# A two-layer hybrid decoder in float32 parts: the compression's first layer in plain float32 from a buffer of its own, two reorderings, and compressed operands padded to 128 rows

## The reference, cut to what matters

```python
def compress(kv, pos_emb, w1, w2, idx):          # 31 blocks of 32 tokens, stride 16
    blocks = kv[:, idx] + pos_emb[None, None, :, None, :]
    blocks = blocks.transpose(0, 1, 3, 2, 4).reshape(bsz, 31, 2, 32 * 64)
    return jax.nn.gelu(blocks @ w1) @ w2          # w1: 2048 x 128, w2: 128 x 64
...
kc, vc = compress(kc, ...), compress(vc, ...)
kc = apply_partial_rope(rms_norm(kc, k_norm[0]), cos_c, sin_c)
p_cmp = masked_softmax(einsum('bqghd,bngd->bghqn', q_c, kc) * scale, valid)
o_cmp = einsum('bghqn,bngd->bqghd', p_cmp, vc)
out   = g0 * o_cmp + g1 * o_slc + g2 * o_win      # o_slc, o_win: over the tokens
x     = x + concat([out, conv_part]) @ w_out
```

## Time and profile before

| | |
|---|---|
| median of three runs | 1798.89 us |
| the profiled execution | 1798.12 us, span 1796.3 us |
| PE busy | 1775.5 us, 99% of the span |
| PE weight loads | 1465.8 us, 82% |
| DVE | 859.3 us, 48% |
| ACT | 598.6 us, 33% |
| POOL | 92.5 us, 5% |
| granted TensorE clock | full in all 40 slices |
| chain that ended last | PE 95%, DVE 3%, ACT 1%, issue 1% |

### The profile page before, as it was taken

How to read it: one execution, slowest core, us unless ns; L and a number is a source line. 1 busy time by engine, 2 the same in 40 slices (tenths; PEclk the granted TensorE clock), 3 DMA queues, 4 the chain that set the end, 5 groups by cost and what they waited for, 6 DMA issues and landing times.

```text
span 1796.3 us, 22196 instructions
## 1 busy us (share of the span) xinstructions
PE 1775.5 (99%) x8164; PEld 1465.8 (82%) x8164; DVE 859.3 (48%) x1104; ACT 598.6 (33%) x838; POOL 92.5 (5%) x81
## 2 busy tenths in 40 slices
PE   8999999999999999999999999999999999999999
PEld 6888888877777878888888888888888888888887
DVE  5544443356788845444443344444432564444322
ACT  5333332235336534333222233232222533332211
POOL 0500000012000011000000000000000000000000
PEclk9999999999999999999999999999999999999999
DMA  6333343324320013333343323333432233333331
GB/s 177 94 93 99 99 115 97 89 75 104 83 82 13 1 47 94 96 102 93 93 125 96 95 82 94 102 96 93 124 97 66 77 94 98 101 93 107 113 96 47
DMA packets 321362, 163.68 MB, mean 91 GB/s; under 512 B 13893, under 2 KB 320041, under 8 KB 321322
## 3 DMA queue, kind: packets, MB, share of 16 engines
q1 hardware_dynamic: 321130, 163.08, 31.5%
q10 hardware_dynamic: 192, 0.08, 0.0%
HBM read 161.04 MB, written 2.10 MB: 91 GB/s over the span
## 4 chain that ended last, share of the span: by engine, by line
PE 95%; DVE 3%; ACT 1%; issue 1%; DMA 0%; SPq 0%; POOL 0%; ACTq 0%; DVEq 0%
PE ps_s L532 20%; PE ps_s L534 20%; PE ps_s L533 20%; PE ps_y L532 9%; PE ps_y L533 9%; PE ps_y L534 9%; PE ps_aux L867 2%; PE ps_y L850 1%; DVE w_lo L1407 1%; PE ps_s L818 1%; PE ps_aux L864 1%; ACT w_hi L1019 1%; PE ps_s L819 0%; PE ps_aux L869 0%; DMA x_in<-in_x 0%
## 5 line engine op out<-in xcount | busy, mean ns | idle before, releaser
L1407 DVE TENSOR_TENSOR w_lo<-raw,w_hi 128x1024 fp32r<-128x1024 f32 (+2 forms) x279 | 368.0, 1319 | 726.4 <-ACT w_hi L1019 725.9
L532 PE MATMUL ps_s<-xg_hi,w_hi 128*128 128x512 f32 x1576 | 618.8, 393 | 0.1
L534 PE MATMUL ps_s<-xg_hi,w_lo 128*128 128x512 f32 x1576 | 613.3, 389 | 0.0
L533 PE MATMUL ps_s<-xg_lo,w_hi 128*128 128x512 f32 x1576 | 613.3, 389 | 0.0
L1019 ACT CAST w_hi<-raw 128x1024 fp32r<-128x1024 f32 (+2 forms) x279 | 312.1, 1119 | 591.9 <-PE ps_s L534 298.1
L532 PEld LDWEIGHTS ps_s<-xg_hi,w_hi 128*128 128x128 f32 x1576 | 295.8, 188 | 65.8 <-issue 2.9
L533 PEld LDWEIGHTS ps_s<-xg_lo,w_hi 128*128 128x128 f32 x1576 | 295.9, 188 | 63.5 <-issue 2.4
L534 PEld LDWEIGHTS ps_s<-xg_hi,w_lo 128*128 128x128 f32 x1576 | 295.8, 188 | 61.9
L532 PE MATMUL ps_y<-act_hi,w_hi 128*128 128x512 f32 x704 | 274.3, 390 | 0.7 <-DVE w_lo L1407 0.7
L534 PE MATMUL ps_y<-act_hi,w_lo 128*128 128x512 f32 x704 | 273.9, 389 | 0.0
L533 PE MATMUL ps_y<-act_lo,w_hi 128*128 128x512 f32 x704 | 273.9, 389 | 0.0
(11 more groups left out here) (314 smaller groups left out, 1078.5 us busy)
## 6 DMA issues: line engine op xcount, KB each, us to landing
raw<-in_ffn_w_gate SPq DMA_DIRECT2D x88, 512.0 KB, 3.9
raw<-in_ffn_w_up SPq DMA_DIRECT2D x88, 512.0 KB, 3.9
raw<-in_ffn_w_down SPq DMA_DIRECT2D x64, 704.0 KB, 4.5
raw<-in_hyb_w_in SPq DMA_DIRECT2D x19, 512.0 KB, 3.8
x_in<-in_x SPq DMA_DIRECT2D x8, 256.0 KB, 6.0
raw<-in_hyb_cmp_w SPq DMA_DIRECT2D x4, 512.0 KB, 4.0
raw<-in_hyb_w_in SPq DMA_DIRECT2D x8, 256.0 KB, 3.3
raw<-in_hyb_w_out SPq DMA_DIRECT2D x16, 128.0 KB, 2.8
```

Source lines behind the costliest of these rows:

```text
L532: mm(bank, hi, x_hi, start=first, stop=False, **kw)
L533: mm(bank, hi, x_lo, start=False, stop=False, **kw)
L534: return mm(bank, lo, x_hi, start=False, stop=last, **kw)
L1407: tt(w_lo[:, n % 2, 0:size], raw[:, n % 4, 0:size], f32(w_hi[:, n % 2, 0:size]), ALU.subtract).then_inc(lo_ready, 1)
```

## The change

- `compress` reads w1 as it came from memory, in plain float32: 16 matmuls of 128x64 instead of 48 of 128x256. w1 has a buffer of its own, `w1_raw` (in the place of `pt_b`), and is loaded by four DMAs that wait for nothing on SP. The four units `U_W1` go, with their splits on ACT and DVE, and so do the splits of the operand (`split_blocks`, `blocks_low`). The units of the loop take their places in the order of splits.
- DVE: scaling and gain of key kw now come ahead of the rotation of ks.
- ACT, in `project_four`: the square of the query now comes ahead of the split of unit n+2 (in the fourth pass, root of kc and square both).
- `vc_t` and `ptc` have 128 rows instead of 32; POOL clears them once, the copies still write 32 rows, and the matmul of line 864 contracts over 128.
- The two small buffers `small` and `small_c` move behind `o_lo`. With that `o_hi` and `o_lo` (and `pt_even`, `pt_odd`) start 320 bytes past a multiple of 512.

```diff
-U_W1 = U_MIX + 7
-U_LOOP = U_W1 + 4
+U_LOOP = U_MIX + 7
...
-            vc_t = mb("vc_t", [NCP, P])
+            vc_t = mb("vc_t", [P, P])
-            ptc = mb("ptc", [NCP, T])
+            ptc = mb("ptc", [P, T])
-            small = mb("small", [P, 2, 10])          # now behind o_lo
-            small_c = mb("small_c", [P, 5, NQ])
-                pt_b = eb("pt_b", [P, 2, 4 * T], F32R)
+                w1_raw = eb("w1_raw", [P, 2, 2, KD * P])
...
# SP
-                load(U_W1 + u, 0, (slot(U_W1 + u), blocks_of(w1)))
+                sp.dma_start(w1_raw[:, u // 2, u % 2, :].rearrange("p (k f) -> p k f", f=P),
+                             blocks_of(w1)).then_inc(w1_landed[u // 2], 16)
...
# PE, compress(c)
-                pe.wait_ge(blk_lo_ready, c + 1)
+                pe.wait_ge(blk_step, 4 * (c + 1))
+                pe.wait_ge(w1_landed[c], 32)
                 for h in range(2):
-                    pe.wait_ge(lo_ready, n + 1)
                     for k in range(KD):
-                        last_mm = three(ps_s[:, p % 4, 0:8 * NCP], w_hi[...], w_lo[...], b_hi, b_lo, ...)
-                    last_mm.then_inc(unit_done, 1)
+                        at = c * 2 * T + (h * KD + k) * 2 * NCP
+                        last_mm = mm(ps_s[:, p % 4, 0:2 * NCP], w1_raw[:, c, h, k * P:(k + 1) * P], qf[:, at:at + 2 * NCP],
+                                     start=h == 0 and k == 0, stop=h == 1 and k == KD - 1)
+                last_mm.then_inc(compressed_by, 1)
...
# ACT
-            split(U_W1)
+            split(U_LOOP)
             split_keys(1)
-            split_blocks(0)
             take_values(0)
-            split(U_W1 + 1)
-            split_blocks(1)
+            split(U_LOOP + 1)
             take_values(1)
-            split(U_W1 + 2)
-            split(U_W1 + 3)
...
-            split(U_LOOP)
             tanh(0)
             split_hidden(0)
-            split(U_LOOP + 1)
             tanh(1)
...
-                    if not (u == 3 and b):
-                        split(n + 2, i)
                     if u == 0:
                         if b:
                             root("kc", DH, 2 * NCP)
                         act.wait_ge(proj_scaled, 10 + 4 * b + 4 * i)
                         square("q3" if b else "q0", sq[:, :], work[:, 0, :], i)
+                    if not (u == 3 and b):
+                        split(n + 2, i)
...
# DVE
-            rope("ks", work[:, 0, :])
             invert("kw", ss[:, :])
             gain_and_norm("kw", R_KN + 2, work[:, 1, :])
+            rope("ks", work[:, 0, :])
...
-            split(U_W1)
+            split(U_LOOP)
...
-            split(U_W1 + 1)
+            split(U_LOOP + 1)
...
-            split(U_W1 + 2)
             keys_low(0)
-            split(U_W1 + 3)
...
-            split(U_LOOP)
             gelu_argument(0)
             gelu_result(0)
             keys_low(1)
-            split(U_LOOP + 1)
...
# POOL
+            nc.gpsimd.memset(vc_t[:, :], 0.0)
+            nc.gpsimd.memset(ptc[:, :], 0.0)
...
-            blocks_low(0)
-            blocks_low(1)
```

More of the change, by code:

```diff
@@ L249, in build @@
             o_lo = mb("o_lo", [P, 4 * T], F32R)
+            small = mb("small", [P, 2, 10])
+            small_c = mb("small_c", [P, 5, NQ])
             w2_hi, w2_lo = (q_parts[:, i, 0:2 * P].rearrange("p (c d) -> p c d", c=2) for i in range(2))
@@ L267, in build @@
         w2_landed = sem("w2_landed")
+        w1_landed = [sem(f"w1_landed{c}") for c in range(2)]
+        compressed_by = sem("compressed_by")
         x_landed = [sem(f"x_landed{i}") for i in range(2 * NQ)]
@@ L317, in build @@
         blk_step = sem("blk_step")
-        blk_hi_ready = sem("blk_hi_ready")
-        blk_lo_ready = sem("blk_lo_ready")
         w2_hi_ready = sem("w2_hi_ready")
@@ L727, in compress @@
                 pe.wait_ge(proj_scaled, p - 3)
-                pe.wait_ge(blk_lo_ready, c + 1)
+                pe.wait_ge(blk_step, 4 * (c + 1))
+                pe.wait_ge(w1_landed[c], 32)
                 for h in range(2):
-                    n = U_W1 + 2 * c + h
-                    pe.wait_ge(lo_ready, n + 1)
                     for k in range(KD):
[L733 to L739, removed]
-                    last_mm.then_inc(unit_done, 1)
+                        at = c * 2 * T + (h * KD + k) * 2 * NCP
+                        last_mm = mm(ps_s[:, p % 4, 0:2 * NCP], w1_raw[:, c, h, k * P:(k + 1) * P], qf[:, at:at + 2 * NCP],
+                                     start=h == 0 and k == 0, stop=h == 1 and k == KD - 1)
+                last_mm.then_inc(compressed_by, 1)
             project(U_MIX, 0, 0, version=1)
@@ L1175, in take_values @@
                 copy(v_t[:, br, :], ps_aux[:, :]).then_inc(aux_free, 1)
-            def split_blocks(c):
-                act.wait_ge(blk_step, 4 * (c + 1))
-                copy(pt_b[:, c, 0:2 * T], qf[:, c * 2 * T:(c + 1) * 2 * T]).then_inc(blk_hi_ready, 1)
             def tanh(c):
@@ L1199, in kc_split @@
                 act.wait_ge(aux_done, AUX.index("t_vc") + 1)
-                copy(vc_t[:, :], ps_aux[0:NCP, 0:P]).then_inc(aux_free, 1)
+                copy(vc_t[0:NCP, :], ps_aux[0:NCP, 0:P]).then_inc(aux_free, 1)
             sums_high(1)
@@ L1297, in take_c @@
                 act.wait_ge(c_pt_done, 2 * j + g + 1)
-                copy(ptc[:, :], ps_stat[0:NCP, :]).then_inc(c_pt_ready, 1)
+                copy(ptc[0:NCP, :], ps_stat[0:NCP, :]).then_inc(c_pt_ready, 1)
             def take_probs(j, s):
@@ L1589, in gelu_argument @@
             def gelu_argument(c):
-                n, p = U_W1 + 2 * c + 1, 7 + c
+                p = 7 + c
                 x, arg = hid[:, 0, c, :], hid[:, 1, c, :]
-                dve.wait_ge(unit_done, n + 1)
+                dve.wait_ge(compressed_by, c + 1)
                 tt(x, ps_s[:, p % 4, 0:2 * NCP], ones[:, 0:2 * NCP], ALU.mult).then_inc(proj_scaled, 1)
@@ L1957, in blocks @@
                            cols[:, at:at + 8].unsqueeze(2).to_broadcast([P, 8, NCP]), ALU.add).then_inc(blk_step, 1)
[L1959 to L1963, removed]
             cosine("ks", 0)
```

## The result

The changed kernel takes 1785.42 us (median of 4 runs, 1785.22 to 1786.02), the kernel before 1798.62 beside it (1797.44 to 1799.77): ratio 0.9928, 95% interval 0.9913 to 0.9944. The profiled runs are 1785.22 and 1798.12. Forecast were 1786.7 for the median and 12.2 us of gain; it is 13.2 by the medians, 12.9 by the profiled runs, and as will be seen 12.05 of that is the change's. The clock granted is 1.00 in every stretch of the stage, and PE is busy 99% as before.

The account below looks back on a forecast made before the run. PE, busy 99% of the span, was taken to bound the kernel. 7.6 - 0.2 + 4.3 + 0.5 = 12.2 us off 1798.12 gave 1785.9, or 1786.7 for the median; range 1784.5 to 1789.

Parts of the forecast that it names:

- Key scale: Rotation of kw: starts 0.85 us earlier, at 407.25, once ks's rotation frees ps_aux; bounds 1.19 and nothing.
- Compression: Compression of w1: weight loads set the pace, 7.1 us for 32 matmuls; the loop's first matmul comes 6.6 earlier.
- Rival 5: Compression: the weights' landing or another new wait holds PE for a few microseconds; around 1795; chance 0.03.
- DVE's chain: Loop's first pass: PE's sum of the query's squares starts 7.6 us earlier, at 437.2, with 0.7 wait remaining.
- The query's square: ACT, loop's first pass: table load of 1.28 behind the wait; square left behind the split would add another 1.05.
- Later passes: Loop's later passes: the reordering puts the query's root some 0.8 later; 0.2 charged for three passes, bounds 0 and 1.5.
- rival 3: Loop: the later split makes PE wait in each pass, up to 1.5 in four places; 6 us back, 1792.7; chance 0.07.
- 128 rows: Attention's matmul in values: padding saves 0.39 a call, 6.3 us over 16 calls; 4.3 kept, bounds 3.1 and 6.3.
- rival 2: Attention: PE's gain is kept whole, and the table load costs no wait; 15.3 us gained, 1783.6; chance 0.14.
- Output at 320: Output projection: the new start address of o_hi and o_lo saves 0.06 eight times, 0.5 us; bounds 0 and 0.7.
- Slower through the clock: Compression and loop: PE's clock falls to 1.2 GHz and the kernel gets slower, 1812; chance 0.03.
- rival 4: Compression, two units and the wait: PE's clock drops from 2.4 to 1.2 GHz for some 25 us; 1812; chance 0.03.

Follow-up runs that it names:

- preload: The changed kernel with ACT loading the table of the square before it waits for the scaled query, in the loop's three passes; 1785.54 us.
- square_back: The changed kernel with the query's square behind ACT's split again, as before the change; 1785.63 us.
- better: The changed kernel with four orders changed (query's square behind the split; three in attention, including DVE's copy ahead of the output's low part); 1781.46 us.

## Why the prediction was right, and where not

- **Key scale, 0.85.** Measured 0.93, with 0.25 of wait left instead of 0.35. What sets the start now is the freeing of `ps_aux`, as said.
- **Compression.** 5.69 for 5.75. A call takes 3.6 us; 64 columns cost the same 0.11 a record as 1 and 128 did, so the columns don't set the pace. That the weight loads do was argued and not tested. w1's loads took 6.8 us to land in the median instead of 4.0, which cost nothing: no wait for `w1_landed` or POOL's clears appears. Rival 5 is out.
- **DVE's chain, 1.0 behind the loop's start.** 1.13. The wait left, forecast as 0.7, is 0.54 by starts (9.52 against the 8.98 of `preload`) and 0.39 as the profile counts it. The chain was right: DVE scales the query 8.91 earlier in the timeline (433.40 for 442.31), 8.07 without the shift.
- **The query's square.** This step failed: "Had the square stayed behind the split, another 1.05 would be added." I left the table load of 1.28 behind the wait in both orders. With the old one the split would have brought it on in ACT's idle time, and 1.05 of split less 1.28 of load makes the square earlier, not later. With the old order the loop's stretch is 0.75 us shorter and the sum of squares starts 0.31 sooner (9.21 for 9.52). The new order is the one part of the change that costs.
- **Later passes, 0.2.** Measured 0.5, inside the bounds; 0.38 of it lies in the first pass (24.01 from its sum of squares to the next, 23.63 before), and `preload` and `square_back` don't have it. It is the mechanism of rival 3 in one place of four, but its cause is the late root, which the exposed table load makes late.
- **128 rows, 0.39 a call, 4.3 kept.** 0.39 and 4.15. The reason for what is not kept, DVE's copy into `pt_odd`, appears where it was put, and `better` gets the rest back. So rival 2 was false for this change, but all but 0.2 of the 6.2 freed was to be had by swapping two instructions of DVE (4.15 and the 1.88 above).
- **Output at 320, 0.5.** 0.65: a block of `o_hi` had lost 0.02, 0.08 for four where the rows gave 0.06. The term's bounds, 0 and 0.7, held.
- **Slower through the clock.** The granted clock was 1.00 through the compression and the loop, so rival 4 did not come about.

The sum of the terms was 12.2 and the change is worth 12.05. The time came 1.3 us under the forecast for two other reasons: the profiled run was 0.84 ahead before the stage began, and its median lies 0.2 above it instead of 0.8. That the sum is so near is partly luck: terms too high by 0.3 in the later passes, 0.15 in attention and 0.06 in the compression stand against three too low by 0.08, 0.13 and 0.15.

## What to carry to other kernels

An instruction's hidden part (here ACT's table load) goes wherever the instruction does that brings it on: put behind a wait, it is paid in full, so load the table ahead of the wait. A gain on a nearly saturated engine is kept only up to the slack of the engine that feeds it; look in the feeding engine's list for an instruction without a waiting reader ahead of one with a reader, and swap them. And where a whole run varies by a microsecond, distances between like instructions in two traces tell edits of a tenth apart.

## What the hardware showed that I had not expected

- The charge for fewer rows is the same for 64 as for 32 (0.63 to the next start, 0.44 with 128). But the four transposes over 24 rows between plain float32 matmuls over 128 rows take 0.35 us from 422.76 to 423.11, no more than four records of 0.11, and the compression behind them keeps its 3.6. So a change of rows isn't charged everywhere; whether the charge needs an fp32r neighbour was not tried.
- A moving operand of fp32r whose tile starts at 0 or 256 modulo 512 bytes costs 0.02 us per three matmuls of 512 columns against one at 64 or 320. Other starts were not tried, nor why.
- When POOL's product and DVE's split ran at once, the one that started no later kept its time and the other was stretched. In the first pass before the change both started at 451.38: POOL took 2.38, DVE 1.21. In the second POOL started at 474.63 and took 1.31, DVE at 474.89 and took 2.13. After the change POOL started at 443.40 and took 1.29, DVE at 443.73 and took 2.04.
